# Prompt attention of a decoder step: the query tiles of a pair of heads from the last to the first

## The reference

```python
s_s = jnp.einsum('bqgpd,bqgkd->bqgpk', qg, k_s) - slope * d_s
p_s = masked_softmax(s_s, d_s >= 0)
o_s = jnp.einsum('bqgpk,bqgkd->bqgpd', p_s, v_s)
# s_w, p_w, o_w likewise over the window; s_c, p_c, o_c over compressed keys
o = g[..., 0:1] * o_c + g[..., 1:2] * o_s + g[..., 2:3] * o_w
```

## Time and profile before

| what | value |
| --- | --- |
| median of 3 runs | 2426.97 us |
| the profiled execution, its own time | 2434.05 us |
| its span | 2432.2 us |
| TensorE busy in the span | 2018.9 us (83%) |
| TensorE weight loads, beside it | 1625.4 us (67%) |
| VectorE busy | 701.6 us (29%) |
| ScalarE busy | 517.2 us (21%) |
| GpSimd busy | 80.8 us (3%) |
| mean granted TensorE clock | 0.877 |

### The profile page before, as it was taken

The page is one execution under the profiler, slowest core; times in us unless marked ns, Lnnn a source line. Parts: engine busy times, 40 slices in busy tenths (PEclk is TensorE's granted clock), DMA queues, the critical chain, the costliest instruction groups (busy, mean ns, idle before and its releaser), DMA issues.

```text
span 2432.2 us, 54912 instructions
## 1 busy us (share of the span) xinstructions
PE 2018.9 (83%) x24332; PEld 1625.4 (67%) x24332; DVE 701.6 (29%) x1935; ACT 517.2 (21%) x1173; POOL 80.8 (3%) x135
## 2 busy tenths in 40 slices
PE   4599996888888674999984999999989974999974
PEld 3376764777776464888873459876657764888863
DVE  3310024556665222101104020137752022011014
ACT  1110112334332011100003110137752021000002
POOL 1000004100000001000000000000000001000001
PEclk8699996989899795999996999979985685999996
DMA  5578718310000234799969342420000152899952
GB/s 194 199 268 283 264 48 281 105 20 12 12 12 9 57 131 182 287 377 381 371 244 288 100 80 81 99 79 2 1 1 1 52 226 93 324 378 377 381 215 76
DMA packets 175627, 400.71 MB, mean 165 GB/s; under 512 B 50966, under 2 KB 112882, under 8 KB 167186
## 3 DMA queue, kind: packets, MB, share of 16 engines
q1 hardware_dynamic: 157234, 345.55, 41.0%
q0 software_dynamic: 11040, 39.85, 4.7%
q10 hardware_dynamic: 7168, 12.59, 1.4%
HBM read 346.47 MB, written 55.68 MB: 165 GB/s over the span
## 4 chain that ended last, share of the span: by engine, by line
PE 71%; DVE 8%; issue 6%; ACT 5%; DMA 4%; DVEq 2%; SPq 1%; POOL 1%; ACTq 0%; POOLq 0%
PE bank L1449 9%; PE bank L406 7%; PE bank L1444 5%; PE bank L1300 5%; PE bank L1462 4%; PE bank L2027 3%; PE bank L1468 3%; PE bank L2078 2%; DMA adaw<-in_ada_w_dram 2%; PE bank L369 2%; PE bank L609 2%; PE bank L2118 2%; PE bank L2146 2%; PE bank L2164 2%; PE bank L2223 1%
## 5 line engine op out<-in xcount | busy, mean ns | idle before, releaser
L1462 PE MATMUL bank<-wd,actT 128*32 128x384 f32 x1536 | 171.6, 488 | 26.6 <-ACT actT L1561 26.6
L1449 PE MATMUL bank<-wg,xsT 128*32 128x128 f32 x1536 | 176.6, 276 | 0.0
L1444 PE MATMUL bank<-wg,xsT 128*32 128x384 f32 x1536 | 174.5, 494 | 1.2 <-ACT xsT L1551 1.2
L1449 PE MATMUL bank<-wu,xsT 128*32 128x128 f32 x1536 | 172.9, 273 | 0.0
L1468 PE MATMUL bank<-wd,actT 128*32 128x256 f32 (+1 forms) x1024 | 172.4, 327 | 0.0
L1449 PEld LDWEIGHTS bank<-wg,xsT 128*32 128x32 f32 x1536 | 169.9, 112 | 2.2
L1444 PE MATMUL bank<-wu,xsT 128*32 128x384 f32 x1536 | 170.8, 486 | 0.0
L1449 PEld LDWEIGHTS bank<-wu,xsT 128*32 128x32 f32 x1536 | 167.7, 110 | 0.0
L406 PE MATMUL bank<-xm,wp 128*128 128x272 f32 x512 | 122.4, 398 | 17.8 <-DVE xm L561 17.8
L1728 DVE TENSOR_TENSOR act<-bank,act 128x384 f32<-128x384 f32 x32 | 17.8, 558 | 397.8 <-PE bank L1449 397.8
L1468 PEld LDWEIGHTS bank<-wd,actT 128*32 128x32 f32 x1024 | 109.6, 110 | 23.3
(11 more groups left out here) (513 smaller groups left out, 4166.1 us busy)
## 6 DMA issues: line engine op xcount, KB each, us to landing
wg<-in_moe_w_gate_dram SPq DMA_DIRECT2D x32, 2048.0 KB, 11.8
wu<-in_moe_w_up_dram SPq DMA_DIRECT2D x32, 2048.0 KB, 17.1
wd<-in_moe_w_down_dram SPq DMA_DIRECT2D x32, 2048.0 KB, 16.7
adaw<-in_ada_w_dram SPq DMA_DIRECT2D x48, 1024.0 KB, 8.0
wp<-in_rwkv_w_rkv_dram SPq DMA_DIRECT2D x24, 512.0 KB, 3.7
xs<-x_slots SPq DMA_DIRECT2D x32, 384.0 KB, 15.5
x_slots<-zeros POOLq DMA_DIRECT2D x21, 512.0 KB, 14.2
y_slots<-zeros POOLq DMA_DIRECT2D x21, 512.0 KB, 13.7
```

The source lines that it names most:

```text
L1444: mm = pe.matmul(ps[32 * j:32 * j + 32, 0:GW], B.xsT[:, k, 32 * j:32 * j + 32], w[:, k, 0:GW], start=k == 0, stop=k == KT - 1)
L1449: mm = pe.matmul(ps[96:128, q * 128:(q + 1) * 128], B.xsT[:, kk, 32 * q:32 * q + 32], w[:, kk, GW:FF], start=kk == 0, stop=kk == KT - 1)
L1462: mm = pe.matmul(bank[4 + b][32 * j:32 * j + 32, 0:384], act_piece(k, j), w[:, k, b * 384:(b + 1) * 384], start=k == 0, stop=k == 3)
```

## The change

The order of the query tiles within a pair is turned round, from 0,1,2,3 to 3,2,1,0, and the places that name the first unit of a pair name tile 3. The steps of the loops, their shifts and the semaphores stay.

```diff
-UNITS = [(j, i, br) for j in range(KT) for i in range(4) for br in range(2)]
+UNITS = [(j, i, br) for j in range(KT) for i in (3, 2, 1, 0) for br in range(2)]
...
         if br == 0:
-            if i == 0:
+            if i == 3:
                 pe.wait_ge(S("ptc_ev"), j + 1)
                 if j >= 1:
                     pe.wait_ge(S("o_ev"), j)
...
-            first = UNITS[s][1:] == (0, 0)
+            first = UNITS[s][1:] == (3, 0)
...
-            if UNITS[s - 3][1:] == (0, 0):
+            if UNITS[s - 3][1:] == (3, 0):
                 cmp_turn(UNITS[s - 3][0])
```

More of the change, by code:

```diff
@@ L2292, in act_kv @@
                 act.activation(B.PT[u % 2][:, h, 0:128 * (i + 1)], bank[4 + h][:, 0:128 * (i + 1)], ACT.Copy).then_inc(S("pt_ev"), 1)
-            if (i, br) == (0, 0):
+            if (i, br) == (3, 0):
                 act.wait_ge(S("ptc_tr"), j + 1)
```

## The result

The changed kernel is slower: 2462.34 us, the median of 4 runs (2457.24 to 2471.13), against 2428.25 for the kernel before in the same comparison. The ratio is 1.0136, with a 95% interval of 1.0101 to 1.0171. The forecast of 2439.8 had the right sign and less than half of the size (12.8 us of the 34.1 between the two medians), and the time lies above the range of 2426 to 2454.

The account below looks back on a forecast made before the run. The prediction took TensorE to bound prompt attention. First pair +1.2, seven longer waits +14.8 and the shorter end -3.2 made +12.8 us on the median of 2426.97: 2439.8, with an 8 in 10 range of 2426 to 2454.

Parts of the forecast that it names:

- TensorE's own work, 21.23 a pair: Prompt attention: of a pair's 22.18 us, 21.23 are TensorE's own work, and the tile order does not change that.
- VectorE's row of 8.39: Start of a pair: VectorE runs 8.39 us without a gap, through the eviction of the third unit, which ends at 10.50.
- the values at 16.25: First value product of a pair, behind ScalarE's store of the old output bank: starts 16.25 us after the pair does.
- the walk: One pair followed engine by engine in order of time: it lasts 24.30 us, 2.12 more, with 8.05 behind the first values.
- The wait of 2.7: TensorE ahead of a pair's first values: waits 2.7 us for the store in place of 0.95, in seven pairs.
- the copy wait of 0.35: TensorE's turn of a pair's second unit: waits some 0.35 us for ScalarE's copy of the first unit.
- The first pair, 23.6: First pair, mostly at the lower clock level: ends at 23.6 us against 22.39 before, +1.2, bounds 0 and +3.
- The sum without a fall of the clock, +12.8: Whole stage: 1.2 for the first pair, 14.8 for seven later stretches, -3.2 at the end of the last pair.
- the clock stays at 1.00: TensorE's granted clock, middle of the stage: stays at 1.00 between 1640 and 1800 despite the waits; this forecast had 0.62.
- The rival: TensorE's clock falls in each pair's new wait: up to 1.7 us each, 11.9 in seven, median 2451.7; chance 0.22.
- The rivals on the other side: Store wait at the pairs' first values: it goes away (-8.7 us, 2418.3, chance 0.08), or stays 0.9 (-2.0, 2425, chance 0.08).

Follow-up runs that it names:

- e4: The kernel before with only ScalarE's store of the old output bank moved ahead of the exponentials; 2425.3 us, ratio 0.9977 to the kernel before.
- e2: The changed kernel with five unread products added on TensorE ahead of the first values of each pair but the first; 2449.25 us, ratio 1.0071 to the kernel before.
- e3: The changed kernel with the compressed branch's minimum and its drain done twice on VectorE; 2469.31 us in one run.
- e6: The kernel before with the compressed branch's minimum done twice on VectorE; 2432.28 us in one run, against 2436.05 for the kernel before beside it.
- e8: The kernel before, ascending tiles, with the store of the old output bank done three times, one after the other; 2454.29 us in one run.
- e5: The kernel before with the query tiles in the order 0, 3, 2, 1; 2445.92 us in one run.
- e9: The changed kernel with two unread products, not five, added in TensorE's wait ahead of the first values; 2446.79 us in one run.
- e1: The changed kernel with ScalarE's store of the old output bank moved ahead of the exponentials; 2437.5 us, ratio 1.0025 to the kernel before.

## Why the prediction was wrong

**TensorE's own work, 21.23 a pair whatever the order: right.** e4 shows it as the length of a pair.

**VectorE's row of 8.39, and the values at 16.25: right.** The row took 8.73 in the pair shown (1633.70 to 1642.43), 8.32 without the odd idle piece. The values start at 16.03, and at 16.35 and 16.39 in the two pairs where VectorE has its odd idle piece of 0.4. With 8.06 behind them (8.05 in the walk) that is a pair of 24.09, seen in e2; the walk had 24.30. e3 and e6 show that the values hang on VectorE's row, in this order and not in the ascending one. The same walk done for the order 0, 3, 2, 1 was right within 0.06 us.

**The wait of 2.7 and the copy wait of 0.35: right in sum.** They are 2.44 and 0.52 in a usual pair, 2.96 against 3.05 (2.44 and 0.79 where VectorE has its odd piece).

**The first pair, 23.6: right** (23.53; its own terms add up to 23.5). What it was compared with wasn't steady. In the ascending order the first pair took 22.39 and 22.69 where the clock rose 18 us after the stage began, and 19.4 in e4 and e8, where it rose after 11. That the term came out at +1.1 is therefore in part luck: against 19.4 it would have been +4. The descending order had the clock up after 7.6 to 7.8 us in each profile. So had the order 0, 3, 2, 1 of e5, which starts with one-tile scores, so it isn't shown which units bring the rise.

**The sum without a fall of the clock, +12.8: right within one us.** e2 gives 197.43 - 185.61 = 11.8 us, counted against a kernel before whose first pair took 22.39.

**The step that failed: the clock stays at 1.00.** I gave the fall 0.22 and made the other case the forecast, on the argument that the gap in rows 7 was slightly longer and this one had work on both sides. That was no evidence: 2.9 us against 2.7 is no difference to build on, and I had no row of a wait of that size with the clock staying up. The trace of the kernel before even had a gap like this one with a fall, right behind the stage, in sample attention. TensorE alone (busy us, clock, DMA share, GB/s), then the row of its timeline that ends the gap:

```profile
1803.00:1804.00 1.00, 0.65 (x8) 1.00 0.00 0
1804.00:1805.00 1.00, 0.00 (x0) 0.75 0.00 0
```

```profile
1806.09 1.08 PE L2193 MATMUL bank<-region_b,region_a 64*32 64x256 f32 x8 [2.43 <-DVE region_a L2482]
```

A gap of 2.43 us, and the clock falls inside it. The runs showed the same in place of the step that failed: the clock came down at all seven waits of 2.44 us. The Trainium skill, "TensorE: Matmul & The Clock Gate", section "Why this matters for your kernels", warns of idle gaps between bursts of matmuls only from a length somewhat above the wait worked out here. The measured waits were shorter still, and the clock fell at all fourteen of them in the changed kernel and e3, so shorter gaps counted here, and the measurement decides.

**And its price was too small.** The rival took three us at half speed from rows 7, at most 1.7 us a pair and 11.9 in all, up to 2451.7. Measured are 17.5, or 2.5 a pair. Rows 7 had been read rightly: that fall was over within 3.4 us, as the next stretch of the same trace shows (columns as in rows 7).

```profile
1326.00:1329.00 3.00, 3.00 (x13) 2.48 (x12) 0.00 (x0) 1.06 (x1) 0.00 (x0) 0.90 1.16 186
```

What failed was to take one fall as the length of all. In the changed kernel the two falls of 3.4 us cost 1.5 to 1.6 us a pair, about what the rival had said, and the five of 6.8 us cost 2.5 to 3.1 where a next pair follows to measure them by (10.54 to 11.18, less 8.06). What decides between the two lengths isn't shown. With 12.8 + 17.5 the sum is 30.3 us, and the stage grew by 29.3. On the median of 2426.97 that is 2457.3; the rest up to 2462.34 is within the spread of the executions.

**The rivals on the other side** needed VectorE's row to be some 2 to 3 us shorter. It was as long as worked out, within 0.1 us.

## What to carry to other kernels

Where several in-order queues work on units of different size, put the large units away from the steps that carry extra work of the pair (here the values started at 14.6 with a small unit there and at 16.0 with the largest), and walk one period on paper with start-to-start times: here that gave the start of the waiting product within 0.3 us. Then look at the idle time of TensorE that the walk leaves. If it has grown from one us to more than two in the middle of dense work, as it did here, count the clock as falling until a run shows otherwise. In these kernels such a fall cost 1.5 to 3.1 us of a pair. The cheapest repair is to release the waiting engine first: moving one store ahead of 1.1 us of exponentials took the kernel before from 22.18 to 21.23 a pair.

## What the runs showed of the hardware

How often the clock fell, by the empty time just ahead of the first values, seven such waits in each kernel: 2.44 us, 14 times of 14 (the changed kernel and e3); 2.13, 6 of 7 (e8); 1.75, 5 of 7 (e5); 1.57, 1 of 7 (e9); 1.12, never (e1); 0.88, never in 14 (the kernel before and e6); 0.28, never (e2). That is what these kernels showed, with their work around the waits; it is no limit for others.

What a fall cost varied. In all five kernels with falls it lasted either 3.4 or 6.8 us, in e8 the two in turns. In the changed kernel and its variants the work behind the wait took 8.06 us when the clock held (e2) and 9.6 to 11.2 when it didn't.

In the first pair TensorE is at the lower level for 7.6 to 18 us although it is busy in nearly all of the time (6.90 of the first 7.00 us in the changed kernel).

Work that nobody reads made the kernel faster: five products of 128x128 by 256 columns in a pair, put where TensorE waits, gave back 17.5 us of stage time (e2 against the changed kernel).
